# The mask of the last attention: from a memset on VectorE to products of one row on TensorE

## What is computed

```python
def diff_attention(h, k, v, w_q, q_norm, lq1, lq2, lk1, lk2, sub_norm, w_o, cos, sin, lambda_init):
    ...
    key_chunk = jnp.arange(S) // CHUNK                      # CHUNK = 64
    def one_block(args):
        qb, bi = args                                       # a block of 128 queries
        scores = jnp.einsum('bhcqd,bhckd->bhcqk', qb, k, preferred_element_type=jnp.float32)
        q_chunk = (bi * Q_BLOCK + jnp.arange(Q_BLOCK)) // CHUNK
        mask = key_chunk[None, :] <= q_chunk[:, None]
        p = jax.nn.softmax(jnp.where(mask, scores, -jnp.inf), axis=-1)
        attn = p[:, :, 0] - lam * p[:, :, 1]
        return jnp.einsum('bhqk,bhkd->bhqd', attn, vf)
```

## Time and profile before

| | |
|---|---|
| median of 3 runs | 3873.72 us (3871.31 to 3874.3) |
| the profiled execution, its time | 3868.01 us |
| its span, first to last instruction | 3866.7 us |
| TensorE busy over the span | 97% |
| VectorE, ScalarE, GpSimd busy | 51%, 35%, 10% |
| the attention of the change | about 3355 to 3448 us |

### The profile page before, as it was taken

The page is one execution under the profiler, slowest core; times in us unless marked ns, Lnnn a source line. Parts: engine busy times, 40 slices in busy tenths (PEclk is TensorE's granted clock), DMA queues, the critical chain, the costliest instruction groups (busy, mean ns, idle before and its releaser), DMA issues.

```text
span 3866.7 us, 44910 instructions
## 1 busy us (share of the span) xinstructions
PE 3753.1 (97%) x18180; PEld 3040.4 (79%) x18180; DVE 1962.8 (51%) x3056; ACT 1335.9 (35%) x2193; POOL 388.3 (10%) x296
## 2 busy tenths in 40 slices
PE   7999999999999998999999999999999999879999
PEld 4868777888887866788888876888877888658888
DVE  5456567755546355544443357534443344474343
ACT  3245443323234334323332236322233223473222
POOL 0000002750000010000010011100020001101000
PEclk8999999999999989999999999999999999899999
DMA  5200012343322201233333332333222332103332
GB/s 211 93 28 1 1 50 85 126 134 120 123 91 73 63 28 39 82 98 98 93 98 98 99 98 77 93 98 98 90 91 88 98 98 93 61 17 98 94 98 92
DMA packets 105821, 329.99 MB, mean 85 GB/s; under 512 B 11536, under 2 KB 13200, under 8 KB 105616
## 3 DMA queue, kind: packets, MB, share of 16 engines
q1 hardware_dynamic: 103024, 320.38, 26.1%
q10 hardware_dynamic: 2592, 6.74, 0.5%
HBM read 324.99 MB, written 2.10 MB: 85 GB/s over the span
## 4 chain that ended last, share of the span: by engine, by line
PE 87%; DVE 4%; ACT 1%; issue 1%; POOL 0%; ACTq 0%; DVEq 0%
PE ps L673 24%; PE ps L674 24%; PE ps L675 24%; PE ps L1514 2%; PE ps L1499 1%; PE ps L1489 1%; PE ps L1490 1%; PE ps L1394 1%; PE ps L1396 1%; PE ps L1395 1%; PE ps L2591 1%; PE ps L2555 1%; PE ps L2589 1%; DVE t L3344 1%; DVE t L843 1%; DVE t L829 1%
## 5 line engine op out<-in xcount | busy, mean ns | idle before, releaser
L673 PE MATMUL ps<-t 128*128 128x512 f32 (+1 forms) x4576 | 1730.9, 378 | 27.4 <-DVE t L843 15.3
L674 PE MATMUL ps<-t 128*128 128x512 f32 (+1 forms) x4576 | 1711.3, 374 | 0.0
L675 PE MATMUL ps<-t 128*128 128x512 f32 (+1 forms) x4576 | 1709.8, 374 | 0.0
L673 PEld LDWEIGHTS ps<-t 128*128 128x128 f32 x4576 | 867.4, 190 | 208.1 <-DVE t L843 23.5
L674 PEld LDWEIGHTS ps<-t 128*128 128x128 f32 x4576 | 868.2, 190 | 154.9 <-issue 6.5
L675 PEld LDWEIGHTS ps<-t 128*128 128x128 f32 x4576 | 867.2, 190 | 152.9
L297 DVE TENSOR_TENSOR t<-t 128x1024 fp32r<-128x1024 f32 (+1 forms) x517 | 649.1, 1256 | 441.4 <-ACT t L288 438.2
L288 ACT ACTIVATE t<-t 128x1024 fp32r<-128x1024 f32 (+1 forms) x517 | 533.2, 1031 | 777.0 <-PE ps L675 674.9
L1258 POOL TENSOR_TENSOR t<-t 128x512 f32<-128x512 f32 x88 | 113.9, 1295 | 1218.0 <-ACT t L1245 1218.0
L1288 DVE SCALAR_TENSOR_TENSOR t<-ps,t 128x512 f32<-128x512 f32 x96 | 66.4, 692 | 236.3 <-PE ps L675 236.3
L1248 ACT ACTIVATE t<-t 128x512 fp32r<-128x512 f32 x88 | 55.6, 632 | 339.9 <-DVE t L1278 339.9
(11 more groups left out here) (375 smaller groups left out, 3299.7 us busy)
## 6 DMA issues: line engine op xcount, KB each, us to landing
t<-w_s_up SPq DMA_DIRECT2D x176, 512.0 KB, 3.5
t<-w_up SPq DMA_DIRECT2D x88, 512.0 KB, 3.6
t<-w_ada SPq DMA_DIRECT2D x160, 256.0 KB, 3.0
t<-w_s_down SPq DMA_DIRECT2D x64, 512.0 KB, 3.5
t<-w_down SPq DMA_DIRECT2D x32, 512.0 KB, 3.6
t<-w_s_down SPq DMA_DIRECT2D x32, 384.0 KB, 3.0
t<-w_ada SPq DMA_DIRECT2D x16, 512.0 KB, 10.6
t<-w_rec_in SPq DMA_DIRECT2D x16, 512.0 KB, 3.6
```

Source lines behind the costliest of these rows:

```text
L673: k.T.matmul(out, wh, hh, start=(i == 0), stop=False)
L674: k.T.matmul(out, wh, hl, start=False, stop=False)
L675: ins = k.T.matmul(out, wl, hh, start=False, stop=(i == len(kts) - 1))
```

## The change

The memset of the hidden square and its wait are taken out of `dve_max`. Instead each of the two score products is followed by a product of one row, 128 columns of weights and 64 columns streamed, that adds to the last 64 keys in the same PSUM bank: the weights are the row MASK (-1e30 for the first 64 queries, 0 for the others), and what is streamed are 64 ones. The score product opens the accumulation and no longer closes it. MASK is written once by two memsets on GpSimd ahead of its part of the rotation, and TensorE waits for them once before the attention. The semaphore `hidden` goes.

```diff
@@ pe_scores
         for c in range(2):
             r = slice(64 * c, 64 * c + 64)
-            ins = k.T.matmul(k.ps[:, 2 * (i % 2) + c, 0:self.nk(i)], self.Q[r, h, q * 128:(q + 1) * 128],
-                             self.KS[r, h, 0:self.nk(i)], start=True, stop=True)
+            b, nk = k.ps[:, 2 * (i % 2) + c, :], self.nk(i)
+            k.T.matmul(b[:, 0:nk], self.Q[r, h, q * 128:(q + 1) * 128], self.KS[r, h, 0:nk], start=True, stop=False)
+            ins = k.T.matmul(b[:, nk - 64:nk], self.masked, k.ones[0:1, 0:64], start=False, stop=True)
         ins.then_inc(self.sc.sem, 1)
@@ dve_max
         k.dve.wait_ge(self.sc.at(i + 1))
-        k.V.memset(k.ps[0:64, s:s + 2, nk - 64:nk], -1e30).then_inc(self.hid.sem, 1)
-        k.dve.wait_ge(self.hid.at(i + 1))
         k.V.tensor_reduce(m[:, 0:2], k.ps[:, s:s + 2, 0:nk], AX.X, ALU.max).then_inc(self.mx.sem, 1)
@@ diff_attention
+        MASK = k.alloc(base, 128)
+        mask = k.event("diff_mask")
...
+                k.G.memset(MASK[0:1, 0:64], -1e30).then_inc(mask.sem, 1)
+                k.G.memset(MASK[0:1, 64:128], 0.0).then_inc(mask.sem, 1)
                 for m in range(8):
                     queries.pool(m)
...
+            attend.masked = MASK[0:1, :]
+            k.pe.wait_ge(mask.at(2))
             attend.pe_program()
```

More of the change, by code:

```diff
@@ L3229, in __init__ @@
         self.ready, self.values_ready, self.free = ready, values_ready, free
-        (self.sc, self.hid, self.mx, self.neg, self.ex, self.rc, self.ratio, self.cm, self.tn, self.kept, self.pv, self.fin,
+        (self.sc, self.mx, self.neg, self.ex, self.rc, self.ratio, self.cm, self.tn, self.kept, self.pv, self.fin,
          self.sq) = (k.event("pair_" + n) for n in (
-             "scores", "hidden", "max", "shift", "exp", "recip", "ratio", "combined", "turned", "kept", "values", "result",
+             "scores", "max", "shift", "exp", "recip", "ratio", "combined", "turned", "kept", "values", "result",
              "square"))
@@ L3361, in end @@
             k.banks.free[b] = t
-        for s in (self.sc, self.hid, self.mx, self.neg, self.rc, self.ratio, self.cm, self.tn, self.kept, self.pv, self.fin,
+        for s in (self.sc, self.mx, self.neg, self.rc, self.ratio, self.cm, self.tn, self.kept, self.pv, self.fin,
                   self.sq):
@@ L3499, in diff_attention @@
             attend.dve_program()
+            mask.past(2)
             t_sq = attend.sq.at(32)
```

## The result

The changed kernel takes 3944.58 us (median of 4 runs, 3934.53 to 3958.69) against 3874.01 before; the ratio is 1.019, 95% interval 1.017 to 1.021. That is 71 us slower, where the forecast was 17 us slower and its range ended at 3900. The profiled execution (3934.53 us, a span of 3933.2) is the fastest of the four; the mean granted clock over the span is 0.965 in it and 0.958 in the slowest one.

A forecast was written before the change was run, and what follows sets the result against it. VectorE was taken as nearly the bound before, TensorE after: 19.6 us for split pairs less 1.6 for the clock gave +18 on the profiled 3868.0, and with the median 5.7 above it 3891 us was predicted, range 3872 to 3900.

The forecast's parts named there:

- What bounds the kernel before: Attention heads of 10.25 us at full clock: VectorE nearly the bound at 9.24 us, with one TensorE passage of 2.43 us.
- A pair costs as one, and a change of rows starts TensorE anew: Attention scores: two score products cost as much as one; each change of row count between neighbours costs about 0.10 us.
- Sizes at full clock: Attention on TensorE: score products 0.42 to 1.06 us by columns, a mask 0.36; a head 12.7 us, bounds 12.3 to 13.2.
- TensorE becomes the bound, VectorE's saving is worth nothing: Per attention head, TensorE needs 12.7 us against VectorE's 8.4, so the 0.8 us saved on VectorE gains nothing.
- The clock: Attention: later half-clock stretches vanish (-6.75 us), the first head's costs 2.7 to 5.5; net -4 to -1.3, taken as -1.6.
- the split at full clock: Eight attention heads with score, mask, score, mask drained at each change: 2.45 us more per head, 19.6 in all (16.4 to 23.6).
- the median 5.7 us above the profiled execution: Whole kernel: profiled execution forecast at 3886, and the median of the runs put 5.7 us above it, at 3891.7.
- Half clock per head: A TensorE-bound attention head at half clock takes some 1.75 times as long as at full clock, 22 us.
- The chances: Whole kernel: slower 0.72, same 0.25, faster 0.03; fresh starts with TensorE the bound had 0.70.
- the rivals with a price of its own: Attention: pair stays together, 3870.5 to 3874 us (0.19); in order without drain, +1 to +10 (0.08); faster, 3863 to 3866 (0.03).

## Why the prediction was wrong

- **What bounds the kernel before:** right. VectorE's chain with one passage over TensorE a head; without the memsets a head is 0.9 us shorter (expected 0.6 to 0.8).
- **A pair costs as one, and a change of rows starts TensorE anew:** right, also for 64 to 1 row, which no row had shown. The Trainium skill, "TensorEngine Tiling (Array Packing)", Key Properties, says that a change of the tiling mode drains TensorE. The runs agree: beside scores of 64 rows, masks of 1, 32 and 128 rows split the pair (heads of 22.96, 22.96 and, at full clock, 12.22 us), masks of 33 and 64 rows do not (9.56 us).
- **Sizes at full clock:** right. Expected for 512, 384, 256 and 128 columns 1.06, 0.85, 0.63, 0.42 us and 0.36 for a mask; the timeline of the changed kernel has 1.05, 0.84, 0.63, 0.42 and 0.36. A whole head was forecast at 12.7 us, and 12.7 is what the estimate from the head of 14.7 us gives. A head with the pair split came to 12.22 us with masks of 128 rows, where the change from the last mask to the transposes is missing (0.1 us four times in my terms).
- **TensorE becomes the bound, VectorE's saving is worth nothing:** right (memset kept: no difference; 77.2 us of waits for L3269).
- **The clock:** this is the step that failed. The prediction said: "In both stages where TensorE was busy throughout the granted clock was 1.00. So I expect the later stretches at half clock to go away", and took -1.6 us. The stage lost 68.1 us. Forecast for the split at full clock were 19.6, and the run with masks of 128 rows shows 16.0 with one change of rows less a pair (32 of 0.1 us); the remaining 49 to 52 us are the half clock: 139.9 us of the stage ran at it, against 34.1 before. With -1.6 in the sum the sign of that term was wrong and its size out by some fifty. This is nearly all of the miss of 54 us; another 4 us come from taking the median 5.7 us above the profiled execution, where it lies 10.1 above it in the changed kernel.
- **Why it failed:** the prediction took TensorE's busy share for what decides the clock. "Busy" in the windows is the time covered by records, whatever their rows. The stages of the earlier trace rows hold other products than a split pair. The second of them mixes products of 128 rows (32 us of busy time; records overlap) with products of 64 and 8 rows (13 us). Three of its groups, with busy time and mean ns:

```profile
L2589 PE MATMUL ps<-t 128*128 128x129 f32 x36 | 8.6, 321 | 0.0
L2591 PE MATMUL ps<-t 64*128 64x129 f32 x34 | 8.3, 323 | 0.0
...
L2521 PE MATMUL ps<-t 8*128 8x512 f32 x8 | 2.3, 640 | 0.0
```

So thin products and changes of rows among products of 128 rows went with a clock of 1.00 there. In the split order products of 64 rows and of one row, one at a time, take 8.8 of a head's 12.7 us by the prediction's own terms. The rows at hand held a warning: the heads of the earlier trace rows have TensorE busy for 69%, 76%, 83% and 70% of their time at clocks of 0.50, 0.78, 0.72 and 1.00, so the busy share did not order the clock in this stage.
- **Half clock per head:** 22 us expected, 22.96 measured, so the price of half clock was right and only its duration was not. A range that let the half clock stay for the whole stage would have had 8 x (22 - 10.25) = 94 us as its far end; I gave no case for it.
- **The chances:** slower had 0.72, and it was slower, but the range did not hold the time. None of the rivals with a price of its own was the case either.

What stays open: what of a product the clock goes by. The runs give points and no rule between them. With the pair split, scores of 64 rows and masks of 1 or 32: half clock for most of the stage; the same scores with masks of 128, or scores of 128 with masks of 1: full clock after one or two heads. With the pair side by side and masks of one row behind it: half clock for two heads with TensorE busy throughout the second (16.8 of 16.8 us), then full.

## What to carry to other kernels

Give a small product that is slipped between others the same division of rows as its neighbours (33 to 64 rows beside 64), padded with zeros or repeated rows if need be: here that turned a loss of 71 us into a small gain, with the same program order. When a change makes TensorE the bound with thin products, price the stage at half clock too, as a case of its own; a stage with "busy" at 100% can run at half clock for most of its time, as this one did. And look at the stage beside the total: the rest of this kernel moved by 15 us over the fourteen profiled executions, more than the mask can give.

## What was not expected of the hardware

- The granted clock was lower where TensorE's busy share was higher: 1.00 at 82% busy with pairs side by side, 0.50 at 100% busy with split pairs, two heads later in the same execution.
- With no change of rows between them, a product on partitions 64 to 127 starts beside the one on 0 to 63 even where the program has another product on 0 to 63 in between (x4 and x4 in the timeline with 64 rows, 1.23 us for all four products with 512 and 64 columns).
- At full clock the two mask products of a pair cost TensorE 0.17 us with 64 rows, and 0.58 us with one row behind the pair. With one row between the scores they cost 1.14 to 1.78 us: 0.36 twice, and the second score product alone (0.42 to 1.06 us).
